# First hybrid layer of a two-block model: the values matmul of a softmax unit is placed after the next unit's transposes and the scores after those, with six visits to TensorE per head pair

## What is computed

```python
def attend(q, k, v):
    s = jnp.einsum('btkgd,bskd->bkgts', q, k).astype(jnp.float32) * (q.shape[-1] ** -0.5)
    p = jax.nn.softmax(s, axis=-1)
    return jnp.einsum('bkgts,bskd->btkgd', p, v)
...
    na_x = neighbourhood_attention(heads(nq, NA_HEADS), heads(nk, NA_HEADS), heads(nv, NA_HEADS),
                                   kc_na, vc_na, na_rpb, rows) * jax.nn.silu(ng)
    gqa_x = gqa_blocks(q_g, k_all, v_all) * jax.nn.silu(gg)
    if need_ctx:
        na_y = attend(heads(cnq, NA_HEADS)[:, :, :, None, :], kc_na, vc_na).reshape(b, l, NA_W) * jax.nn.silu(cng)
        gqa_y = attend(qc_g, kc_g, vc_g).reshape(b, l, GQA_W) * jax.nn.silu(cgg)
```

## Time and profile before

| what | value |
|---|---|
| median of 3 runs | 1943.93 us (1940.58 to 1944.17) |
| the profiled execution | 1944.93 us |
| its span (first to last instruction) | 1943.2 us |
| TensorE busy | 1921.3 us, 99% of the span |
| VectorE, ScalarE, GpSimd busy | 67%, 47%, 18% |
| mean granted clock of TensorE | 0.995 of full speed |
| na pairs of this layer | about 61 to 192 us of the span |
| gqa pairs of this layer | about 384 to 540 us of the span |

### The profile page before, as it was taken

How to read it: one execution, slowest core, us unless ns; L and a number is a source line. 1 busy time by engine, 2 the same in 40 slices (tenths; PEclk the granted TensorE clock), 3 DMA queues, 4 the chain that set the end, 5 groups by cost and what they waited for, 6 DMA issues and landing times.

```text
span 1943.2 us, 31968 instructions
## 1 busy us (share of the span) xinstructions
PE 1921.3 (99%) x11894; PEld 1657.9 (85%) x11894; DVE 1304.7 (67%) x1966; ACT 915.2 (47%) x1435; POOL 358.2 (18%) x360
## 2 busy tenths in 40 slices
PE   8999999999999999999999999999999999999998
PEld 6777888877788788998998888998888888998887
DVE  5675677455444665546667886799867886579874
ACT  5444332244433544435555554765544554555543
POOL 1101211011122011201114320013302330204320
PEclk9999999999999999999999999999999999999999
DMA  8432335221233342343456566456666566555663
GB/s 316 136 106 87 109 109 184 77 66 56 83 106 98 118 147 88 110 145 109 126 175 183 186 189 190 149 170 191 185 190 203 191 185 191 166 163 180 189 186 117
DMA packets 79435, 289.27 MB, mean 149 GB/s; under 512 B 8912, under 2 KB 9168, under 8 KB 79312
## 3 DMA queue, kind: packets, MB, share of 16 engines
q1 hardware_dynamic: 73152, 265.36, 43.5%
q0 software_dynamic: 5728, 21.50, 3.4%
q10 hardware_dynamic: 432, 0.72, 0.1%
HBM read 286.49 MB, written 1.05 MB: 148 GB/s over the span
## 4 chain that ended last, share of the span: by engine, by line
PE 89%; issue 8%; DVE 1%; ACT 1%; POOL 0%; DMA 0%; DVEq 0%; POOLq 0%; ACTq 0%; SPq 0%
PE bank L2645 24%; PE bank L2638 15%; PE bank L2639 13%; PE bank L2640 13%; PE bank L2651 13%; PE bank L2880 2%; PE bank L2863 2%; PE bank L2849 2%; PE bank L2920 1%; PE bank L2905 1%; PE bank L2693 1%; PE bank L2770 1%; PE bank L2941 0%; POOL stats L1610 0%; PE bank L2817 0%
## 5 line engine op out<-in xcount | busy, mean ns | idle before, releaser
L2007 DVE TENSOR_TENSOR w_lo<-raw,w_hi 128x1024 fp32r<-128x1024 f32 x484 | 625.1, 1294 | 236.6 <-ACT w_hi L1713 226.2
L1713 ACT ACTIVATE w_hi<-raw 128x1024 fp32r<-128x1024 f32 x484 | 510.4, 1059 | 500.8 <-PE bank L2640 285.2
L2638 PE MATMUL bank<-h,w_hi 128*128 128x512 f32 (+1 forms) x1312 | 464.6, 354 | 3.8 <-DVE w_lo L2007 1.5
L2639 PE MATMUL bank<-h,w_hi 128*128 128x512 f32 (+1 forms) x1312 | 444.5, 339 | 0.0
L2640 PE MATMUL bank<-h,w_lo 128*128 128x512 f32 (+1 forms) x1312 | 444.0, 338 | 0.0
L2645 PE MATMUL bank<-h,w_hi 128*128 128x512 f32 x1408 | 357.0, 393 | 0.3 <-issue 0.3
L2638 PEld LDWEIGHTS bank<-h,w_hi 128*128 128x128 f32 x1312 | 248.8, 190 | 54.2 <-issue 24.6
L2645 PEld LDWEIGHTS bank<-h,w_hi 128*128 128x128 f32 x1408 | 253.4, 189 | 46.6 <-issue 0.3
L2640 PEld LDWEIGHTS bank<-h,w_lo 128*128 128x128 f32 x1312 | 249.0, 190 | 28.1
L2639 PEld LDWEIGHTS bank<-h,w_hi 128*128 128x128 f32 x1312 | 249.5, 190 | 22.1
L2651 PEld LDWEIGHTS bank<-h,w_lo 128*128 128x128 f32 x1408 | 193.7, 190 | 13.5
(11 more groups left out here) (267 smaller groups left out, 2378.8 us busy)
## 6 DMA issues: line engine op xcount, KB each, us to landing
raw<-in_weights SPq DMA_DIRECT2D x484, 512.0 KB, 3.6
m<-in_modulation POOLq DMA_DIRECT2D x24, 512.0 KB, 4.4
early<-in_first SPq DMA_DIRECT2D x10, 512.0 KB, 13.4
spare<-in_modulation POOLq DMA_DIRECT2D x8, 512.0 KB, 4.5
bias<-in_rpb POOLq DMA_DIRECT2D x8, 384.0 KB, 4.7
early_o<-in_first SPq DMA_DIRECT2D x4, 512.0 KB, 16.1
x<-in_tokens SPq DMA_DIRECT2D x3, 512.0 KB, 6.9
work<-in_first SPq DMA_DIRECT2D x2, 512.0 KB, 15.4
```

Of the source, the lines that this page charges most:

```text
L1713: nc.scalar.activation(w_hi[:, n % SPLIT, :], raw[:, t % RAW, :], ACT.Copy).then_inc(hi_ready, 1)
L2007: dve.tensor_tensor(w_lo[:, t % RAW, :], raw[:, t % RAW, :], w_hi[:, SPLIT_NO[t] % SPLIT, :].bitcast(F32), ALU.subtract).then_inc(lo_ready, 1)
L2638: nc.tensor.matmul(dst, w_hi[:, SPLIT_NO[t] % SPLIT, at], hi, start=start, stop=False, skip_group_check=shared)
L2639: nc.tensor.matmul(dst, w_hi[:, SPLIT_NO[t] % SPLIT, at], lo, start=False, stop=False, skip_group_check=shared)
```

## The change

The change moves V(u-1) behind T(u) and S(u+1) in one fill, puts an empty fill between such fills, drops one of the two empty fills behind S0, and adds an empty fill ahead of the last V. The fills of a pair are now: S0; nothing; T0 S1; nothing; T1 S2 V0; nothing; T2 S3 V1; nothing; T3 V2; nothing; V3; turn_out; turn_low. There are again 13 entries, of which six use TensorE. T(u) stands one entry earlier for every unit, V3 where it stood. Since V(u-1) now follows T(u), ACT's copy of T(u) gets a wait for V(u-1), on a new semaphore, or on `o_full` where V(u-1) is the last unit of the pair before. The fold of the first ada section is due one part later than before, since its sums now end one fill earlier.

```diff
@@ ada_sum
-                self.later(2, lambda: self.ada_fold(section))
+                self.later(2 if section else 3, lambda: self.ada_fold(section))
@@ softmax_units
+            if blocks == 4 and not u.last:
+                u.v_n = s.count("values_over")
...
+        def with_values(u):
+            def run():
+                both(u, after[u])()
+                if not u.first:
+                    values(units[units.index(u) - 1])()
+            return run
+
         if blocks == 4:
-            slots = [lambda: scores(units[0]), rest, rest]
+            slots = [lambda: scores(units[0]), rest]
             for u in units:
-                slots += [both(u, after[u]), values(u)]
-            return slots + [lambda: turn_out(g), lambda: turn_low(g)]
+                slots += [with_values(u), rest]
+            return slots + [values(units[-1]), lambda: turn_out(g), lambda: turn_low(g)]
@@ block_kernel
+        last_unit = {}
+        for st in steps:
+            if st.kind == "turn_probs":
+                last_unit[st.u.n] = st.u
+
+        def values_over(n):
+
+            u = last_unit[n]
+            return (o_full, u.g.o_use + 1) if u.last else (values_used, u.v_n + 1)
@@ turn_probs_step on ScalarE
+                if u.n and u.g.blocks == 4:
+                    act.wait_ge(*values_over(u.n - 1))
@@ values_step on TensorE
                 if u.last:
                     ins.then_inc(o_full, 1)
+                elif u.v_n is not None:
+                    ins.then_inc(values_used, 1)
```

More of the change, by code:

```diff
@@ L261, in __init__ @@
                  o_use=None, outs=None, part=None, s_use=None, slot=None, src=None, t=None,
-                 t_use=None, t_uses=None, tile=None, turn=None, u=None, up=None, what=None, out=None):
+                 t_use=None, t_uses=None, tile=None, turn=None, u=None, up=None, what=None, out=None, v_n=None):
+        self.v_n = v_n
         self.kind, self.n = kind, n
@@ L1287, in block_kernel @@
         o_full = sem("o_full")
+        values_used = sem("values_used")
         o_free = sem("o_free")
```

## The result

The changed kernel takes 1945.81 us (median of 20 executions, 1943.10 to 1950.22) beside 1943.9 of the kernel before (20 executions, 1938.14 to 1944.43). The ratio is 1.0015 with a 95% interval of 1.0009 to 1.0021: 1.9 us more, where +1.85 was predicted. Measured again later, it was 1945.69 beside 1943.82 (ratio 1.0011, 1.0002 to 1.002). The profiled execution is the one of 1945.81 us, span 1944.0 us.

A forecast was written before the change was run, and what follows sets the result against it. TensorE, busy 99% of the span, bounds the kernel, through shape borders and pauses. Terms -3.2 + 0.7 + 3.85 + 0.8 - 0.3 = +1.85 us gave 1946.8 profiled, 1945.8 median; range 1941.5 to 1950.0.

The forecast's parts named there:

- bounds that the prediction set itself: By its terms na pairs get 1.95 us longer, wrong under 1 or over 3; gqa pairs 0.1 shorter, wrong if off by over 1.
- the pause of pair 3: TensorE ahead of T0 in na pair 3: the pause grows by the whole fill, 2.07 us, to 3.1.
- the rotation: TensorE at the rotation in gqa pair 0: a new pause of 0.8 us behind DVE's L2408, between nothing and 2.07.
- the fold: Ahead of T3 in na pair 3: the fold now comes behind T3 V2, so a 0.32 us bank wait goes, -0.3.
- Joins: S2 V0 and S3 V1 adjacent in eight pairs, 16 joins: gain 0.20 us each, 3.2 in all, between 0 and 5.6.
- the rival in which the step from S to V is free: At the S–V joins: worth all they can be, gain 5.6 us, time 1943.4; chance 0.08.
- T0 pauses, pairs 0 to 2: TensorE ahead of T0 in na pairs 0, 1, 2: new waits for scaled probabilities of 0.84, 0.47, 0.47 us.
- Lost joins with the spread: In gqa pairs 1 and 2, V no longer stands directly behind the spread: two joins lost, 0.35 each, +0.7 us.
- ACT's new wait at nothing: ACT's copy of T(u) waits for V, delaying exponentials of units 2 and 3 and evacuations: costed at nothing.
- the 1947.5: Rival: the clock falls to half in na pair 3's long pause, costing 1.7 us, time 1947.5; chance 0.15.
- Later units: Rival: T1 in four na pairs pauses 0.96 us, or T2 behind the copy's wait: +3.8, in all 1949.6; chance 0.12.
- the pauses stay away: Rival: T0's pauses in pairs 0 to 2 and the rotation's do not come, 1943.2; without pair 3's too, 1941.1; chance 0.05.

The follow-up runs named there:

- t0_early_alone: The kernel before with T0 one fill earlier and the fold one part later, no joined V, no new ACT wait: 1950.25 us, ratio 1.0032.
- t0_back: The change with a second empty fill behind S0 again, every T where the kernel before had it, T, S, V still joined: 1943.51 us, ratio 1.000.
- t0_early_again: The unchanged kernel of t0_early_alone profiled once more, for the clock: 1950.03 us in its one execution.
- v_first: The change with T at the places of the kernel before, V ahead of T and S in the visit, no ACT wait on V: 1942.46 us, ratio 0.9996.
- best_chain: The change with decay tables one product later, the conditioning sum behind the scaling, first head scaled before the second's reciprocal: 1941.0 us, ratio 0.9985 to the kernel before.

## Why the prediction came out right

- **Time.** 1945.8 predicted, 1945.81 and 1945.69 measured; the difference is +1.9 us for the +1.85 of the sum. By profile stretches it is +1.5 (+0.8 to +1.5 over three profiles). In the first profile the na part is +1.52 us for +1.95, the gqa part -0.03 for -0.1, both inside the bounds that the prediction set itself. Without the noisy last column the gqa part is +0.29, where the same terms give +0.3. So the sum is right, but that it is right to 0.1 us is luck: the pause of pair 3, the rotation and the fold were each off by 0.16 to 0.38, and S0 of na pair 0 alone stands 0.34 later in the profile after.
- **Joins, 0.20 each.** Right, by the steps above and by the change against t0_early_alone (0.41 to 0.45 per pair). So the rival in which the step from S to V is free, with a gain of 5.6 us, is refuted.
- **T0 pauses, pairs 0 to 2.** 0.84, 0.47, 0.47 predicted, 0.78, 0.44, 0.50 measured. Pair 0 then is 0.78 - 0.40 = +0.38 (measured +0.43), pairs 1 and 2 +0.04 and +0.10 (measured +0.08, +0.15).
- **T0 pause, pair 3.** Mis-sized: 2.07 for the whole fill, measured 1.72. "None of this moves" was the wrong step. DVE's low part ahead of the bias waits for ACT, which is busy with the tables, and ACT had in them a wait of 0.39 us for its own first table. After the change that wait is gone, and the table's successor starts 0.61 behind it in place of 0.91. ACT of the change:

```profile
159.38 0.52 ACT L1877 ACTIVATE abs_dif<-con 128x384 f32<-128x384 f32 x1
159.99 0.62 ACT L1885 ACTIVATE decay_s<-abs_dif,log_g 128x384 f32<-128x384 f32 x1
```

and DVE, the low part and the scaling:

```profile
163.29 1.23 DVE L2031 TENSOR_TENSOR w_lo<-raw,w_hi 128x1024 fp32r<-128x1024 f32 x1 [2.49 <-ACT w_hi L1735]
...
167.49 0.21 DVE L2354 RECIPROCAL row_stat<-row_stat 128x1 f32<-128x1 f32 x2
167.68 0.88 DVE L2359 TENSOR_SCALAR work<-work,row_stat 128x512 f32<-128x512 f32 x2
```

The wait for ACT is 2.49 us, 0.30 less than in the earlier trace rows. ACT of t0_early_alone, in the kernel before's code:

```profile
158.16 0.62 ACT L1861 ACTIVATE decay_s<-abs_dif,log_g 128x384 f32<-128x384 f32 x1 [0.39 <-ACT abs_dif L1853]
```

It keeps its 0.39, and its T0 pause is 2.04 us longer than before (3.11 for 1.07), the 2.07 of the forecast. The earlier T0 is thus not what removes the wait. With the tables in their old place, every profile of a kernel in which ACT waits for V lacks it (the change three times, t0_back), and every profile of a kernel without that wait on ACT has it (before, t0_early_alone, t0_early_again, v_first). T0's pause in t0_back is shorter by the same 0.3 (0.79 for 1.07). What in those kernels removes it stays open.
- **Rotation.** 0.8 predicted, 0.42 measured, for two reasons of the same size. The product on DVE ended 6.6 us behind S1 (392.45), not 6.9: the low part followed the scaling without waiting for ACT. And TensorE was there at +6.4, not +6.1: the prediction took 0.97 us for the spread, which is what a group of this shape takes behind another of it; alone between products it takes the 1.23 that the prediction reads for V. Against that, 0.15 us passed between the end on DVE and the start on TensorE, which was put at nothing.
- **Fold.** 0.3 predicted, the idle time of the earlier trace rows; counted in starts it gives 0.16 more back, 0.46. Pair 3 on: 1.72 - 0.40 - 0.46 = +0.86, as measured.
- **Lost joins with the spread.** 0.35 each predicted, 0.38 and 0.40 in t0_early_alone, where gqa pairs 1 and 2 lose them and gain nothing. With the joins they should then be even; they are 0.08 to 0.09 longer. The squares' sum (L2929) got other neighbours too, which no term had; how much of it that is was not tried.
- **ACT's new wait at nothing.** Right: no T or V of units 1 to 3 waits, and V's wait for ACT's copy is 0.5 us in one place, as before.
- **Rivals.** The clock did not fall in the change in three profiles, so the 1947.5 did not come; but in the kernel of t0_early_alone it did, with a pause 0.3 us longer, for 2.9 and 1.5 us (1.7 and its double in the forecast). The Trainium skill, "TensorE: Matmul & The Clock Gate", section "HAM oscillation — how this bites in real kernels", says that a long enough idle stretch between bursts sends the clock back; the two profiles of that kernel, with pauses of 3.11 and 3.09 us, agree. Later units did not come late in the change, and do in t0_back. That the pauses stay away is what best_chain brings about by its edits: 1941.0, for the rival's 1941.1.

## What to carry to other kernels

Moving a small group beside another gained just the slow steps at its borders (0.20 us of some 2 us), while moving its consumer a fill earlier exposed a chain on DVE that had been hidden: price both, then shorten the chain before moving anything. Look at what stands in a chain without belonging to it: a table of another group, an unrelated sum, and the second head's reciprocal together cost more here (4.4 us in the na columns, 324.43 to 320.04) than all the joins gave (3.2). A pause of the array is to be read as its own length plus the danger to the clock.

## What the runs showed that was not expected

- A wait for an instruction of the same engine (0.39 us on ACT) was there in some kernels and gone in others that do not touch it, and passed through two engines onto TensorE's pause, 0.30 us. Why is open.
- Pauses of 3.11 and 3.09 us brought the clock to 0.50, for 6.8 and some 3 us; 2.79 us did not in three profiles. The same kernel with nearly the same pause thus paid 2.9 in one execution and 1.5 in another.
- The way out of V costs 0.06 us in front of T and 0.11 us in front of a wide product, although both use the full array.
- The start of the program, up to the first S0, varies by 4.0 us between executions (58.28 to 62.31), more than the change is worth, and in the traces with the granted clock at 16 to 28 us; a stretch of the trace between two fixed instructions repeats within 0.7 us.
